# The experts' gate table moves to DRAM and is filled by indirect adding transfers

## The chip, the cores and the metric

The kernel runs on one core of one Trainium2 chip, in one launch. The metric is the device time of that core in microseconds (us). TensorE is called PE, VectorE DVE, ScalarE ACT, GpSimd POOL, and SyncE SP, as in the profile.

## The reference

Two transformer blocks, one after the other, on 256 tokens of width 2048, in float32. What matters here is the last part of the second block, `peer`: 16,384 experts, numbered by a pair of keys (128 x 128), of which each token takes 16 for each of 8 heads.

```
q  = x @ wq                                  # 8 heads x 256
s1, s2 = q[..., :128] @ keys1.T, q[..., 128:] @ keys2.T
v1, i1 = top_k(s1, 16);  v2, i2 = top_k(s2, 16)
top_s, pos = top_k(v1[:, None] + v2[None, :], 16)      # 16 of 256 candidates
expert = (i1 * 128 + i2)[pos]
gate   = softmax(top_s)
z      = x . u[expert]                       # 128 picks for each token
out    = sum over picks of gelu(z) * gate * v[expert]
```

Both kernels compute it densely. They work out z for all 16,384 experts as a matrix product (`u`), take gelu, multiply by a gate table G of [16,384 experts x 256 tokens] that is zero except at the picked places (an expert picked by two heads of one token has the sum of both gates), and multiply by all of `v`.

## The kernel before

**Stream.** All large weights come as one stream of 902 units of [128 x 1024] floats, 512 KB each. Two units are a pair. SP loads unit n into one of four slots (`raw`) as soon as the low part of unit n-4 is made (L601). ACT rounds the unit to fp32r (`w_hi`, `split_hi`, L474), DVE makes the rest (`w_lo`, `split_lo`, L483), and PE multiplies with both. ACT may write slot s only when PE has done unit n-4. The order of work is written out by hand on each engine; the helper `ahead` splits the pair that comes two after the one that PE is at.

**The u part.** Experts come in NB = 128 blocks of 128. For one block PE takes a pair: for each of the two units, 8 products of 512 columns with `w_hi` (L532) and 8 of 256 with `w_lo` (L539) (`halves_out`). ACT copies the low half of the bank (`low_half`, L545), DVE adds the other half (`add_halves`, L550), ACT takes gelu. Block pairs of PE must wait for the sum of the block two before (`wait_summed`), since two banks take turns.

**Where the blocks are made.** `wqu`: the queries of a head and two blocks of u, 8 times; POOL adds the halves (`add_copied`). `u_decode`: 16 blocks, while DVE turns the top-16 lists into experts and gates, unit by unit between its splits (`more`); at its end the gates, the first and the second index stand in `PICK`. `u_gates`: 64 blocks, while the gate table is made. `u_late`: 32 blocks. `v`: 128 pairs, 24 products of 512 columns each (`expert`, L2571 to L2573). In `v`, ACT and DVE split the next block of gated activations into `expert_hi_t` and `expert_lo_t`, and DVE makes `w_lo`.

**The gate table.** G takes all of the large buffer `big` (128 KB of each partition), as [second index x first index x token]. PE turns `PICK` (6 transposes, L2530) so that the 128 picks of a token lie on partitions. For each token POOL makes a one-hot matrix of the second index (L678), DVE a one-hot matrix of the first index times the high and the low part of the gate (L2005), and PE multiplies them (L2540, [128 x 128] by 256 columns). ACT copies the low half into G (L1145) and DVE adds the high half (L1999). Four tokens go with each of the 64 pairs of `u_gates`, between the products with `w_hi` and with `w_lo` of the second unit:

```
for s in range(4):
    pe.matmul(GATE_BANKS[n][s // 2][...], hot[:, s, :], weighted[:, s, :, :]..., start=True, stop=True)
```

**The activations.** Since G fills `big`, gelu of the first 96 blocks is stored in DRAM (`z_kept`, by ACT's queue) and read back (L1163, L1195) into two buffers `GB` in `u_late` and in the first half of `v`, where DVE multiplies it into G (L2037, L2063). The last 32 blocks are multiplied at once (L2034).

Of the kernel before, what the change touches and what calls it, by code (L numbers as in the profile page):

```python
# [28 lines left out]
F32 = mybir.dt.float32  # L29
# [6 lines left out]
P = 128  # L36
S = 256
# [28 lines left out]
SLOT_N = PH * PK  # L66

# [3 lines left out]
         ("wqu", 4 * PH), ("u_decode", 2 * PH), ("u_gates", S // 4), ("u_late", NB // 4), ("v", NB)]  # L71
EARLY = 3 * NB // 4
LATE = NB - EARLY
# [11 lines left out]
for _name, _count in [("conv", 4 * CONV_J), ("rnn", 2 * KT), ("heads", 2 * H2), ("u_decode", 2 * PH), ("u_gates", S // 4),  # L85
                      ("u_late", LATE)]:
    HALVED[_name] = _n
    _n += _count
# [5 lines left out]
for _name, _count in [("ident", P), ("iota", P), ("band", TT * 2 * P), ("causal", TT * S), ("cos", TT * HALF),  # L94
                      ("sin", TT * HALF)]:
    CONST[_name] = (_n, _n + _count)
    _n += _count
# [37 lines left out]
def build(nc, stream, x, p_t, rows, consts, params, rg_w, ukv, keys_t, out):  # L135
    ctx = ExitStack()
    with ctx:
# [24 lines left out]
        with nc.sbuf_tensor("expert_act", [P, 2, 2, S], F32R) as expert_act:  # L162
            pass
        weighted = sb("weighted", [P, 4, 2, P], F32R)
        with nc.sbuf_tensor("below_hot", [P, CONST["causal"][0]], F32), \
                nc.sbuf_tensor("hot", [P, 4, P], F32R) as hot:
            pass
# [4 lines left out]
        slot_t = sb("slot_t", [P, 3, S])  # L172
# [3 lines left out]
        z_kept = nc.dram_tensor("z_kept", (EARLY, P, S), F32, kind="Internal").ap()  # L176
# [91 lines left out]
        PICK = at(16896, 3 * SLOT_N * TT).rearrange("p (a h t k) -> p a h t k", a=3, h=PH, t=TT)  # L268
        PICKT = at(17664, 3 * SLOT_N * TT).rearrange("p (a t h k) -> p a t h k", a=3, h=PH, t=TT)
# [4 lines left out]
        G = big[:, :].rearrange("p (b t) -> p b t", b=NB)  # L274

        first_index = slot_t[:, 0, :]
        second_index = par[:, 0:S]
        gate_hi = slot_t[:, 1, :]
        gate_lo = slot_t[:, 2, :]
        GATE_BANKS = [[banks[0], banks[1]], [banks[4], banks[5]]]  # L280
        GZ = c("band").rearrange("p (s n) -> p s n", s=2)
        GB = c("causal").rearrange("p (s n) -> p s n", s=2)

# [28 lines left out]
        idx8 = stat[:, 8:16]  # L312
# [120 lines left out]
        picks_ready = sem("picks_ready")  # L433
        picks_turned = sem("picks_turned")
        slots_kept = sem("slots_kept")
        hot_turn = sem("hot_turn")
        hot1 = sem("hot1")
        hot2 = sem("hot2")
        hot_used = [sem(f"hot_used{n}") for n in range(4)]
        gate_low = sem("gate_low")  # L440
        gate_kept = [sem(f"gate_kept{n}") for n in range(2)]
        gelu_ready = [sem(f"gelu_ready{n}") for n in range(2)]
        z_saved = [sem(f"z_saved{n}") for n in range(2)]
        z_back = [sem(f"z_back{n}") for n in range(2)]
        early_ready = [sem(f"early_ready{n}") for n in range(2)]
# [77 lines left out]
        def halves_out(pe, pair, odd, bank, units=(0, 1), between=None, paced=None):  # L523

            for u in units:
# [8 lines left out]
                if u and between:  # L534
                    between()
# [20 lines left out]
        def tokens_out(pe, part, i, per, k0, outs, fills, acts=None, units=range(8)):  # L556

            high, low = acts or (act_hi, act_lo)
            for uu in units:
# [5 lines left out]
                for kk in range(2):  # L565
# [13 lines left out]
        primed = [y_made, z_saved, early_ready, scored, rg_done, logits_made, hot2, hot_used, conv_b_used,  # L579
                  conv_h_used, conv_gate_used, qi_scored, rel_used, xc_ready, th_used, gr_used, head_mixed, ps_made,  # L580
                  ps_used, act_ready, qkvg_taken_s, qkvg_taken_v, probs_kept, mix_used, added, gated, rel_ready,
                  rg_exp, k_kept, v_kept, p_exp, ga_tanh, p_kept, ps_kept, gate_kept, gelu_ready]
# [42 lines left out]
        def _(pool):  # L625
# [6 lines left out]
            pool.sem_inc(pool_summed, 4)  # L632

            with pool.Fori(0, TT) as t:
                with pool.Fori(0, KVH) as g:
# [5 lines left out]
                                     .rearrange("p o n -> p (o n)")).then_inc(staged, 1)  # L641

# [20 lines left out]
            with pool.Fori(0, PH) as h:  # L663
# [3 lines left out]
                for n in range(2):  # L667
                    add_copied(Z_HALVES[:, n, 0:S], Z_HALVES[:, n, :], h * 4 + (2 + n))
            pool.wait_ge(slots_kept, 3)
# [19 lines left out]
        def _(act):  # L689
# [369 lines left out]
            def save_early(b2, n, block):  # L1059

                act.wait_ge(z_saved[n], b2 * 16 + 1)
                act.wait_ge(pool_summed, block + 5)
                act.activation(GZ[:, n, :], Z_HALVES[:, n, 0:S], ACT.Gelu).then_inc(gelu_ready[n], 1)
                act.wait_ge(gelu_ready[n], b2 + 2)
                act.dma_start(z_kept[bass.ds(b2 * 2 + n, 1), :, :].rearrange("o p n -> (o p) n"), GZ[:, n, :])\
                   .then_inc(z_saved[n], 16)
# [1654 lines left out]
```

## Time and profile before

| | |
|---|---|
| median of 3 runs | 2732.92 us (2732.72 to 2734.38) |
| span of the profiled execution, first to last instruction | 2730.6 us |
| PE busy | 2707.6 us (99%) |
| DVE busy | 1890.1 us (69%) |
| ACT busy | 1391.3 us (51%) |
| POOL busy | 358.1 us (13%) |
| DMA | 522.17 MB, mean 191 GB/s |

The profiled execution's own time outside the profiler is not listed; its span stands 2.3 us below the median of the runs, which also takes in what lies before the first and after the last instruction. Busy time of an engine is the union of its instructions. Matmuls overlap, so the time of one (0.39 us for 512 columns) is longer than the step from one to the next (0.23 us).

### The profile page before, as it was taken

The numbers are of one execution on the slowest core, as the hardware profiler recorded it, in microseconds if no ns is written. First come the engines' busy times: TensorE is split into PE (matmuls) and PEld (weight loads), VectorE is DVE, ScalarE is ACT, GpSimd is POOL, SyncE is SP. The second block draws the span as 40 slices with busy tenths as digits, with TensorE's granted clock in tenths as the row PEclk, the third lists the DMA queues.
The fourth block names the chain that finished last, engine by engine and source line by source line (L and its number), as shares of the span: only waits on it lengthen the run. The fifth ranks groups of instructions, "written<-read, shape, count | busy, mean of one in ns | idle before, by whom it ended". The sixth has DMA issues, their size and how long they took to land.

```text
span 2730.6 us, 48285 instructions
## 1 busy us (share of the span) xinstructions
PE 2707.6 (99%) x14430; PEld 2332.0 (85%) x14430; DVE 1890.1 (69%) x3047; ACT 1391.3 (51%) x2118; POOL 358.1 (13%) x422
## 2 busy tenths in 40 slices
PE   8999999999999999999999999999999999999998
PEld 7888888898888888888888888888888888888887
DVE  6666665668986666479997888886665555555555
ACT  6455445556665444465455555554544444444444
POOL 0000000000001111011104666660000000000000
PEclk9999999999999999999999999999999999999999
DMA  6544455454554444555565555556666666655564
GB/s 256 192 155 160 148 196 184 176 215 162 172 176 159 155 159 140 200 193 195 196 199 202 197 190 197 194 196 206 211 215 217 218 213 218 212 194 192 194 239 156
DMA packets 162487, 522.17 MB, mean 191 GB/s; under 512 B 18048, under 2 KB 42880, under 8 KB 161408
## 3 DMA queue, kind: packets, MB, share of 16 engines
q1 hardware_dynamic: 131472, 478.35, 51.0%
q10 hardware_dynamic: 30960, 43.14, 4.5%
q8 instruction: 29, 0.48, 0.1%
q14 instruction: 26, 0.21, 0.0%
HBM read 504.63 MB, written 16.78 MB: 191 GB/s over the span
## 4 chain that ended last, share of the span: by engine, by line
PE 94%; DVE 3%; ACT 1%; issue 1%; DMA 0%; SPq 0%; ACTq 0%; DVEq 0%
PE bank L532 31%; PE bank L539 16%; PE bank L2571 8%; PE bank L2573 8%; PE bank L2572 8%; PE bank L572 4%; PE bank L574 4%; PE bank L573 4%; PE bank L2540 1%; PE bank L2373 1%; PE bank L2368 1%; DVE w_lo L483 1%; PE bank L506 1%; PE bank L507 1%; PE bank L508 1%
## 5 line engine op out<-in xcount | busy, mean ns | idle before, releaser
L483 DVE TENSOR_TENSOR w_lo<-raw,w_hi 128x1024 fp32r<-128x1024 f32 x902 | 1095.0, 1224 | 694.7 <-ACT w_hi L474 683.4
L474 ACT ACTIVATE w_hi<-raw 128x1024 fp32r<-128x1024 f32 x902 | 952.1, 1060 | 943.1 <-PE bank L539 359.8
L532 PE MATMUL bank<-act,w_hi 128*128 128x512 f32 x3840 | 975.8, 396 | 2.3 <-DVE big L1420 1.1
L532 PEld LDWEIGHTS bank<-act,w_hi 128*128 128x128 f32 x3840 | 692.6, 189 | 133.7 <-issue 7.2
L539 PEld LDWEIGHTS bank<-act,w_lo 128*128 128x128 f32 x3840 | 520.0, 191 | 33.1
L539 PE MATMUL bank<-act,w_lo 128*128 128x256 f32 x3840 | 535.8, 282 | 0.0
L2571 PE MATMUL bank<-w_hi,expert_act 128*128 128x512 f32 x1008 | 392.6, 389 | 0.1
L2573 PE MATMUL bank<-w_hi,expert_act 128*128 128x512 f32 x1008 | 392.5, 389 | 0.0
L2572 PE MATMUL bank<-w_lo,expert_act 128*128 128x512 f32 x1008 | 392.4, 389 | 0.0
L678 POOL TENSOR_SCALAR hot<-cst,stat 128x128 fp32r<-128x128 f32 x256 | 255.1, 1011 | 129.1 <-PE bank L2540 128.7
L2571 PEld LDWEIGHTS bank<-w_hi,expert_act 128*128 128x128 f32 x1008 | 189.3, 188 | 39.5 <-DVE cst L550 0.5
L2573 PEld LDWEIGHTS bank<-w_hi,expert_act 128*128 128x128 f32 x1008 | 189.3, 188 | 39.2
L2572 PEld LDWEIGHTS bank<-w_lo,expert_act 128*128 128x128 f32 x1008 | 189.3, 188 | 39.1
L572 PE MATMUL bank<-w_hi,act 128*128 128x512 f32 x320 | 126.0, 394 | 1.5 <-DVE w_lo L483 0.8
L574 PE MATMUL bank<-w_hi,act 128*128 128x512 f32 x320 | 124.8, 390 | 0.0
L573 PE MATMUL bank<-w_lo,act 128*128 128x512 f32 x320 | 124.6, 389 | 0.0
L684 POOL TENSOR_TENSOR big<-big 128x1024 f32<-128x1024 f32 x2 | 5.8, 2878 | 874.9 <-DVE big L2078 874.9
L2005 DVE SCALAR_TENSOR_TENSOR weighted<-cst,slot_t 128x256 fp32r<-128x256 f32 x256 | 116.0, 511 | 0.0
L646 POOL TENSOR_TENSOR big<-big 128x256 f32<-128x256 f32 x16 | 11.1, 696 | 485.0 <-DVE big L550 485.0
L572 PEld LDWEIGHTS bank<-w_hi,act 128*128 128x128 f32 x320 | 60.1, 188 | 15.7 <-DVE w_lo L483 1.3
L574 PEld LDWEIGHTS bank<-w_hi,act 128*128 128x128 f32 x320 | 60.1, 188 | 12.6
L573 PEld LDWEIGHTS bank<-w_lo,act 128*128 128x128 f32 x320 | 60.1, 188 | 12.1
(332 smaller groups left out, 2518.1 us busy)
## 6 DMA issues: line engine op xcount, KB each, us to landing
raw<-in_stream SPq DMA_DIRECT2D x902, 512.0 KB, 3.7
z_kept<-cst ACTq DMA_DIRECT2D x96, 128.0 KB, 2.1
cst<-z_kept ACTq DMA_DIRECT2D x96, 128.0 KB, 4.0
big<-in_ukv ACTq DMA_DIRECT2D x16, 512.0 KB, 4.6
big<-in_rows ACTq DMA_DIRECT2D x3, 1024.0 KB, 5.5
big<-in_x SPq DMA_DIRECT2D x2, 1024.0 KB, 9.7
big<-in_rg_w ACTq DMA_DIRECT2D x1, 2048.0 KB, 11.2
x_kept<-big ACTq DMA_DIRECT2D x1, 2048.0 KB, 8.3
```

The lines of the kernel that those rows point to most:

```text
L474: act.activation(w_hi[:, s, :], raw[:, s, :], ACT.Copy).then_inc(hi_ready, 1)
L483: dve.tensor_tensor(w_lo[:, s, :], raw[:, s, :], w_hi[:, s, :].bitcast(F32), ALU.subtract).then_inc(lo_ready, 1)
L532: pe.matmul(bank[:, :], w_hi[:, s, kk * P:(kk + 1) * P], act2[:, k, :, :].rearrange("p a n -> p (a n)"), start=(k == 0), stop=False)
L539: mm = pe.matmul(bank[:, 0:S], w_lo[:, s, kk * P:(kk + 1) * P], act_hi[:, k, :], start=False, stop=(k == KT - 1))
L572: pe.matmul(outs[t], a_hi, hi, start=(k == 0), stop=False)
L573: pe.matmul(outs[t], a_hi, lo, start=False, stop=False)
L574: mm = pe.matmul(outs[t], a_lo, hi, start=False, stop=(k == KT - 1))
L678: pool.tensor_scalar(hot[:, s % 4, :], iota, idx8[:, s:s + 1], None, ALU.is_equal)\
L2005: dve.scalar_tensor_tensor(out=weighted[:, s, :, :], in0=iota.unsqueeze(1).broadcast_to([P, 2, P]), scalar=first_index[:, bass.ds(tok, 1)] ...
L2571: pe.matmul(o, a_hi, hi, start=first, stop=False, skip_group_check=True)
L2572: pe.matmul(o, a_hi, lo, start=False, stop=False, skip_group_check=True)
L2573: mm = pe.matmul(o, a_lo, hi, start=False, stop=False, skip_group_check=True)
```

## The change

The table of gates is a DRAM tensor `g_kept` of 128 x 128 x 256 floats (16.8 MB), one float for each expert and token.

* **Zeroing.** POOL clears a tile of [128 x 1024] once. In the attention of the first block, in each of the 8 turns of POOL's loop, it issues 4 stores of 512 KB of that tile, 32 in all, into `g_kept`.
* **Index and gate.** DVE works out `SLOT_INDEX` = (first index * 128 + second index) * 256 + token and `SLOT_GATE`. PE's transposes, DVE's three copies to `PICKT` and ACT's four copies are gone.
* **Filling.** POOL issues 256 indirect transfers, one for each head, half of the tokens and place in the top 16. Each takes one gate from each of the 128 partitions and adds it to the float of `g_kept` at that partition's index. All 32 transfers of a head must have landed before the next head's first.
* **Activations.** gelu(z) of every block stays in `big` (`z_block`); `z_kept` is gone, with its 96 stores and 96 loads on ACT's queue.
* **Gating.** POOL loads the gate block (128 KB) of each of the 128 blocks into one of two buffers `GB`. DVE multiplies it in (`gate_block`) two blocks at a time: the first two ahead of its turn 46 of the 48 of `u_rest`, the next two in that turn, and all others in `v`.
* **Stages.** `u_gates` (64 pairs) and `u_late` (32) become `u_rest` (96 pairs), without the one-hot products. The order of the blocks changes so that blocks 16 to 31 are made beside the queries and 0 to 15 in `u_decode`.

The diff, cut to its core:

```
-         ("wqu", 4 * PH), ("u_decode", 2 * PH), ("u_gates", S // 4), ("u_late", NB // 4), ("v", NB)]
+         ("wqu", 4 * PH), ("u_decode", 2 * PH), ("u_rest", NB - 4 * PH), ("v", NB)]
...
+        SLOT_INDEX = slot_t[:, 0, :].bitcast(U32)
+        SLOT_GATE = slot_t[:, 1, :]
+        g_zero = g_kept.rearrange("(p c n) o -> c p (n o)", p=P, n=ZERO_W)
+        g_block = g_kept.rearrange("(b p n) o -> b p (n o)", b=NB, p=P)
...
 # POOL
+            pool.memset(zeros[:, :], 0.0).then_inc(zero_made, 1)
+            pool.wait_ge(zero_made, 1)
             with pool.Fori(0, TT) as t:
                 with pool.Fori(0, KVH) as g:
...
+                    for q in range(ZERO_DMAS // (TT * KVH)):
+                        pool.dma_start(g_zero[bass.ds(u * (ZERO_DMAS // (TT * KVH)) + q, 1), :, :]
+                                       .rearrange("o p n -> (o p) n"), zeros[:, :]).then_inc(zeroed, 16)
...
-            with pool.Fori(0, S // 8) as i:
-                pool.wait_ge(hot2, i * 8 + 1)
-                pool.tensor_copy(idx8, second_index[:, bass.ds(i * 8, 8)]).then_inc(g_step, 1)
-                pool.wait_ge(g_step, i + 1)
-                for s in range(8):
-                    pool.wait_ge(hot_used[s % 4], i * 2 + s // 4 + 1)
-                    pool.sem_inc(hot_turn, 1)
-                    pool.tensor_scalar(hot[:, s % 4, :], iota, idx8[:, s:s + 1], None, ALU.is_equal)\
-                        .then_inc(hot2, 1)
+            pool.wait_ge(zeroed, 16 * ZERO_DMAS)
+            pool.wait_ge(slots_ready, TT)
+            for h in range(PH):
+                if h:
+                    pool.wait_ge(scattered, 16 * TT * PK * h)
+                for i in range(h * TT * PK, (h + 1) * TT * PK):
+                    pool.indirect_dma_start(g_kept, bass.IndirectOffsetOnAxis(ap=SLOT_INDEX[:, i:i + 1], axis=0),
+                                            SLOT_GATE[:, i:i + 1], None, compute_op=ALU.add).then_inc(scattered, 16)
+            pool.wait_ge(scattered, 16 * TT * PK * PH)
+            for n in range(2):
+                pool.dma_start(GB[:, n, :], g_block[n, :, :]).then_inc(g_back[n], 16)
+            with pool.Fori(1, NB // 2) as i:
+                for n in range(2):
+                    pool.wait_ge(act_ready[n], i)
+                    pool.dma_start(GB[:, n, :], g_block[bass.ds(i * 2 + n, 1), :, :].rearrange("o p n -> (o p) n"))\
+                        .then_inc(g_back[n], 16)
...
 # ACT
+            def rest_turn(i, first=False):
                 for n in range(2):
+                    ahead(split_hi, act, "u_rest", i, 2, n)
+                    wait_summed(act, block_of("u_rest", i, 2, n - 1))
+                    act.wait_ge(unit_done, 2 * pair_of("u_rest", i, 2, n) + 2)
+                    low_half(act, z_block(i * 2 + (4 * PH + n)), banks[2 + n])
+                    gelu(2 * PH - 1 if first and not n else i * 2 + (4 * PH + n - 1))
+            def expert_hi(b, n, i, done):
+                act.wait_ge(unit_done, done)
+                act.wait_ge(act_ready[n], i + 1)
+                act.activation(expert_hi_t[:, n, :], z_block(b), ACT.Copy).then_inc(eh_ready, 1)
...
 # DVE
-            step(dve.tensor_tensor(PICK[:, 2, :, :, :].rearrange("p h t k -> p (h t) k"), cv,
+            step(dve.tensor_tensor(SLOT_GATE.rearrange("p (n k) -> p n k", k=PK), cv,
                                    crec.unsqueeze(2).broadcast_to([P, PH * TT, PK]), ALU.mult))
+            step(dve.scalar_tensor_tensor(out=picked[1], in0=picked[0], scalar=float(KEYS), in1=picked[1],
+                                          op0=ALU.mult, op1=ALU.add))
             step.wait()
-            for a in range(3):
-                ins = dve.tensor_copy(PICKT[:, a, :, :, :].rearrange("p t h k -> p h t k"), PICK[:, a, :, :, :])
+            for t in range(TT):
+                dve.tensor_scalar(SLOT_INDEX.rearrange("p (h t k) -> p h t k", h=PH, t=TT)[:, :, t, :],
+                                  PICK[:, 1, :, t, :], float(S), c("token")[:, t:t + 1], ALU.mult, ALU.add)\
+                   .then_inc(slots_ready, 1)
...
+            def gate_block(b, n, i):
+                dve.wait_ge(gelu_ready, b + 1)
+                dve.wait_ge(g_back[n], i * 16 + 16)
+                z = z_block(b)
+                dve.tensor_tensor(z, z, GB[:, n, :], ALU.mult).then_inc(act_ready[n], 1)
...
+            with dve.Fori(0, REST // 2 - 2) as i:
+                rest_turn(i)
+            dve.wait_ge(gelu_ready, 4 * PH)
+            for n in range(2):
+                gate_block(n, n, 0)
+            rest_turn(REST // 2 - 2)
+            for n in range(2):
+                expert_lo(n, n, n + 1)
+                gate_block(2 + n, n, 1)
+            rest_turn(REST // 2 - 1)
...
+            with dve.Fori(0, NB // 2 - 2) as i:
                 for n in range(2):
                     next_expert(i, n)
+                    gate_block(i * 2 + (4 + n), n, i + 2)
...
 # PE
-            for a in range(3):
-                pe.wait_ge(picks_ready, a + 1)
-                for t in range(TT):
-                    pe.transpose(banks[4 + a][:, t * P:(t + 1) * P],
-                                 PICKT[:, a, t, :, :].rearrange("p h k -> p (h k)"),
-                                 ident).then_inc(picks_turned, 1)
...
-            with pe.Fori(0, S // 8) as i:
-                for n in range(2):
-                    pe.wait_ge(gelu_ready[n], i + (2 * PH + 1))
-                    halves_out(pe, pair_of("u_gates", i, 2, n), odd_of("u_gates", n), banks[2 + n], between=lambda: four_tokens(i, n))
-            with pe.Fori(0, LATE // 2) as i:
+            with pe.Fori(0, REST // 2) as i:
                 for n in range(2):
-                    wait_summed(pe, block_of("u_late", i, 2, n - 2))
-                    halves_out(pe, pair_of("u_late", i, 2, n), odd_of("u_late", n), banks[2 + n])
+                    wait_summed(pe, block_of("u_rest", i, 2, n - 2))
+                    halves_out(pe, pair_of("u_rest", i, 2, n), odd_of("u_rest", n), banks[2 + n])
```

## Rows read from the trace of the kernel before

**Rows 1.** The page: span, busy time of PE, and the chain that ended last.

```profile
span 2730.6 us, 48285 instructions
...
PE 2707.6 (99%) x14430; PEld 2332.0 (85%) x14430; DVE 1890.1 (69%) x3047; ACT 1391.3 (51%) x2118; POOL 358.1 (13%) x422
...
PE 94%; DVE 3%; ACT 1%; issue 1%; DMA 0%; SPq 0%; ACTq 0%; DVEq 0%
```

**Rows 2.** Busy time by stretch: attention; u_gates; u_late; halves of v.

```profile
core 0: us, PE busy (x) PEld busy (x) DVE busy (x) ACT busy (x) POOL busy (x), PEclk, DMA share, GB/s
...
141.00:332.00 191.00, 191.00 (x1163) 167.22 (x1162) 128.72 (x200) 94.70 (x173) 11.92 (x16) 1.00 0.45 157
...
1463.00:1851.00 388.00, 387.96 (x2303) 345.33 (x2304) 332.44 (x572) 215.75 (x383) 257.73 (x283) 1.00 0.55 194
1851.00:2026.00 175.00, 174.84 (x1004) 153.88 (x1003) 111.38 (x158) 88.38 (x127) 0.00 (x0) 1.00 0.62 212
2026.00:2376.00 350.00, 349.95 (x1545) 289.68 (x1544) 200.29 (x259) 157.02 (x195) 0.00 (x0) 1.00 0.64 216
```

**Rows 3.** PE in order of time, one pair of u_gates apart: start, duration.

```profile
1602.67 0.64 PE L2540 MATMUL bank<-weighted,hot 128*128 128x256 f32 x4
...
1608.73 0.64 PE L2540 MATMUL bank<-weighted,hot 128*128 128x256 f32 x4
```

**Rows 4.** PE in order of time, one pair of u_late apart.

```profile
1903.05 2.00 PE L532 MATMUL bank<-act,w_hi 128*128 128x512 f32 x8
...
1908.64 2.00 PE L532 MATMUL bank<-act,w_hi 128*128 128x512 f32 x8
```

**Rows 5.** PE in order of time: transposes, start of u_gates, start of v.

```profile
1443.11 2.00 PE L532 MATMUL bank<-act,w_hi 128*128 128x512 f32 x8
1444.95 1.11 PE L539 MATMUL bank<-act,w_lo 128*128 128x256 f32 x8
1445.91 0.82 PE L2530 MATMUL bank<-cst,big 128*128 128x128 f32 x6
1446.48 2.10 PE L532 MATMUL bank<-act,w_hi 128*128 128x512 f32 x8
...
1457.75 2.00 PE L532 MATMUL bank<-act,w_hi 128*128 128x512 f32 x8
...
2025.96 0.40 PE L2571 MATMUL bank<-w_hi,expert_act 128*128 128x512 f32 x1
```

**Rows 6.** DVE in order of time: the last steps of the decoding.

```profile
1433.31 0.42 DVE L1981 TENSOR_TENSOR big<-big,stat 128x256 f32<-128x256 f32 x1
...
1433.77 0.70 DVE L1985 COPY big<-big 128x256 f32<-128x256 f32 x3
```

**Rows 7.** One line each: one-hot on POOL, and POOL's smallest copy.

```profile
L678 POOL TENSOR_SCALAR hot<-cst,stat x256: 601/843/1647, 1449.1 to 1842.1; 128x128 fp32r<-128x128 f32 x128
...
L673 POOL COPY stat<-par x32: 189/190/192, 1448.6 to 1831.8; 128x8 f32 x32
```

**Rows 8.** One line each: DMA issues of ACT's queue, store and load.

```profile
L1135 ACTq DMA_DIRECT2D z_kept<-cst x64: 339/343/356, 1469.0 to 1850.1; - x64
...
DMA to landing us min/median/max: 1.8/2.0/3.2
...
DMA to landing us min/median/max: 2.0/4.2/5.0
```

**Rows 9.** The page: DMA queues: packets, MB, share of 16 engines.

```profile
q1 hardware_dynamic: 131472, 478.35, 51.0%
q10 hardware_dynamic: 30960, 43.14, 4.5%
```

**Rows 10.** In order of time: low part made, and the split four units on.

```profile
1898.85 1.23 DVE L483 TENSOR_TENSOR w_lo<-raw,w_hi 128x1024 fp32r<-128x1024 f32 x1 [0.59 <-ACT w_hi L474]
...
1908.84 1.06 ACT L474 ACTIVATE w_hi<-raw 128x1024 fp32r<-128x1024 f32 x1 [0.76 <-PE bank L539]
```

**Rows 11.** Stream loads, issue to landing; POOL's waits in the attention.

```profile
DMA to landing us min/median/max: 3.0/3.7/11.3
...
POOL big L639 <- PE bank L2224: 153.2, 7, 24.7
```

**Rows 12.** Groups: DVE's gate multiplication in v.

```profile
L2063 DVE TENSOR_TENSOR big<-cst,big 128x256 f32 x64 | 26.8, 418 | 0.0
```

More of the change, by code:

```diff
@@ L84 @@
 _n = 0
-for _name, _count in [("conv", 4 * CONV_J), ("rnn", 2 * KT), ("heads", 2 * H2), ("u_decode", 2 * PH), ("u_gates", S // 4),
-                      ("u_late", LATE)]:
+for _name, _count in [("conv", 4 * CONV_J), ("rnn", 2 * KT), ("heads", 2 * H2), ("u_decode", 2 * PH),
+                      ("u_rest", REST)]:
     HALVED[_name] = _n
@@ L1057, in keep_early, with early_gelu @@
                 copy_halves(Z_HALVES[:, n, :], banks[2 + n], pair, block, before)
[L1059 to L1061 removed]
+            def early_gelu(b2, n, block):
                 act.wait_ge(pool_summed, block + 5)
[L1063 to L1066, printed above, removed]
+                act.wait_ge(added[1], 9)
+                z = z_block(b2 * 2 + (2 * PH + n))
+                act.activation(z, z, ACT.Gelu).then_inc(gelu_ready, 1)
             def router_turn(h, first=False):
@@ L1115, in _ @@
-            early_turn(0, first=True)
+                    low_half(act, z_block(i * 2 + n), banks[2 + n])
+                    if not (first and not n):
+                        gelu(i * 2 + (n - 1))
+            decode_turn(0, first=True)
             with act.Fori(1, PH // 2) as i:
-                early_turn(i)
+                decode_turn(i)
             act.wait_ge(pick_diff, 1)
             act.activation(CV, CV, ACT.Exp).then_inc(pick_exp, 1)
-            with act.Fori(PH // 2, PH - 1) as i:
-                early_turn(i)
@@ L1138, in gates_turn @@
-            def gates_turn(i, first=False):
-                for n in range(2):
-                    ahead(split_hi, act, "u_gates", i, 2, n, units=(0,))
-                    if not (first and not n):
-                        save_gelu(i, n - 1)
-                    for half in range(2):
-                        act.wait_ge(hot_used[2 * half + 1], i * 2 + n + 2)
-                        act.activation(G[:, :, bass.ds(i * 8 + (4 * n + 2 * half), 2)],
-                                       GATE_BANKS[n][half].rearrange("p (t a b) -> p a b t", t=2, a=2)[:, 1, :, :],
-                                       ACT.Copy).then_inc(gate_low, 1)
-                    ahead(split_hi, act, "u_gates", i, 2, n, units=(1,))
-                    act.wait_ge(unit_done, 2 * pair_of("u_gates", i, 2, n) + 2)
-                    act.wait_ge(z_saved[n], i * 16 + (32 * PH + 1))
-                    low_half(act, GZ[:, n, :], banks[2 + n])
@@ L1173, in expert_hi @@
[L1173 to L1185 removed]
+            with act.Fori(PH // 2, PH) as i:
+                decode_turn(i)
@@ L1187, in next_experts @@
+            rest_turn(0, first=True)
+            with act.Fori(1, REST // 2 - 1) as i:
+                rest_turn(i)
+            for n in range(2):
+                expert_hi(n, n, 0, 2 * FIRST["u_rest"])
+            rest_turn(REST // 2 - 1)
+            wait_summed(act, block_of("u_rest", REST // 2 - 1, 2, 1))
+            gelu(NB - 1)
             def next_experts(i):
@@ L1926, in next_low @@
                 if u:
-                    add_halves(dve, GZ[:, pair % 2, :], banks[2 + pair % 2], block_of("u_decode", 0, 2, pair))
+                    add_halves(dve, Z[:, pair, :], banks[2 + pair % 2], block_of("u_decode", 0, 2, pair))
             def more(count=1):
@@ L2011, in gates_turn @@
-            def gates_turn(i, last=False):
-                for n in range(2):
-                    ahead(split_lo, dve, "u_gates", i, 2, n, units=(0,))
-                    if not (last and n):
-                        four_tiles(i, n + 1)
-                    ahead(split_lo, dve, "u_gates", i, 2, n, units=(1,))
-                    add_halves(dve, GZ[:, n, :], banks[2 + n], block_of("u_gates", i, 2, n))
-                    add_gates(i, n)
-            four_tiles(0, 0)
-            with dve.Fori(0, S // 8 - 1) as i:
-                gates_turn(i)
@@ L2023, in _, with rest_turn @@
[L2023 to L2037 removed]
+            def rest_turn(i):
+                for n in range(2):
+                    ahead(split_lo, dve, "u_rest", i, 2, n)
+                    add_halves(dve, z_block(i * 2 + (4 * PH + n)), banks[2 + n], block_of("u_rest", i, 2, n))
```

224 lines of the change are left out of this document (49 added, 175 removed).

## The prediction

> **What bounds the kernel now.** The page comes first: PE is busy 2707.6 of 2730.6 us and makes 94% of the chain that ended last [rows 1]. So only what leaves PE's own list, or makes PE wait, moves the time. The table by stretches says the same of the stages in question: in u_gates PE is busy 387.96 of 388 us, in u_late 174.84 of 175, in the first half of v 349.95 of 350, and the granted clock is 1.00 in all of them, the higher of the two levels (2.4 GHz) [rows 2]. DVE comes nearest, with 332 of 388 us in u_gates and 111 of 175 in u_late. POOL works 258 us in u_gates and nothing after it. The sum is made against the span of 2730.6 us; the median of the runs, 2732.92, lies 2.3 us above it, and I carry that over unchanged.
>
> **What leaves PE.** A pair of u_gates takes 1608.73 - 1602.67 = 6.06 us, a pair of u_late without one-hot products 1908.64 - 1903.05 = 5.59 [rows 3, 4]. With 64 pairs that is 64 x 0.47 = 30.1 us. The same from the ends: from the first product of u_gates to the first of v are 2025.96 - 1457.75 = 568.2 us [rows 5]; 96 pairs of 5.59 are 536.6, so 31.6 us go if all 96 run at the pace of u_late. The 1.5 us between the two are the start of u_gates, where PE waits for the first one-hot tiles, and the passage to u_late, where ACT waits for its last store; both causes are removed, and I take 31.6. The six transposes stretch one unit of 2.79 us (half a pair) from 1443.11 to 1446.48, 3.37 us, so 0.6 more goes [rows 5]. Sum: 32.2 us off PE.
>
> **What leaves the other engines.** On DVE 256 tiles and 128 additions, on ACT 128 copies, 192 DMA issues of 0.34 us [rows 8], on POOL 256 one-hots of 0.6 to 1.6 us [rows 7]. Worth nothing: PE covers them. Should PE's cover have been incomplete, u_late (same u work, DVE at 64%) shows that the lighter load keeps PE's pace.
>
> **What is added on DVE and ACT.** Three index operations of 128 to 256 elements take the place of three copies of together 0.70 us [rows 6]: nothing, and the list is ready at about 1434.8. ACT's low half now comes behind the second split in u_decode, as it does in u_late, where PE still has its 5.59. In v, DVE does one multiplication of 0.42 us for each of the 128 pairs [rows 12]; before it did one in each of the first 64 and PE did not wait there (349.95 of 350). In the second half it is new, but makes the load that of the first half: nothing. DVE also loses u_late's two multiplications a pair.
>
> **What is added on POOL and the DMA queues: gate blocks.** 128 loads of 128 KB. The same size landed in 4.2 us from ACT's queue, at most 5.0 [rows 8]. A buffer comes free at one multiplication and is needed again two pairs (about 11 us) later. Even with 3 us more for an issue from POOL, an allowance of mine, it fits. If not, DVE waits, with the next w_lo behind it, and PE behind that. Nothing is taken; a price if cover fails is 128 / 2 x 1 us for each us by which a load is over 10.
>
> **Zeroing.** 16.8 MB in 8 bursts of 2 MB between 141 and 332 us, where the DMA share is 0.45 and PE has no idle time [rows 2]. POOL waits up to 24.7 us a turn there for PE [rows 11]; behind its four issues are queued the two copies of the next turn, for which the attention scores on PE wait. Four issues at 0.34 us are 1.4 us, at 4.2 us each 17: under 24.7 both ways. The stream has slack: the low part of a unit ends at 1900.1, which releases SP's next load, and the split that needs it starts at 1908.8 [rows 10], so 8.7 us against a median landing of 3.7 [rows 11]. A burst would have to double the landing time. Bounds: 0 and, at 3 us a burst, 24 us. I take 1 us, near the lower, as 5 us of slack stand against it.
>
> **The 256 indirect adding transfers: the term that decides.** No row of this trace shows a DMA issued by POOL. First the time they have. They start at 1434.8. DVE meets the first gate block ahead of turn 46, when PE begins pair 92 of u_rest: u_rest starts at 1457.75 - 0.6 = 1457.2, so 1457.2 + 92 x 5.59 = 1971.5. Behind the waiting multiplication are queued the w_lo of pairs 94 and 95 and the sums that free PE's banks. The weights of pairs 92 and 93 are already split, so PE goes on for 11.2 us; two multiplications and a w_lo take 2.1 of these. The deadline is about 1980.5. From 545.7 us go one load of 4.2 and eight drains (one for each head) of a store's 2.0 us [rows 8], which leaves 525.5 us, or 2.05 us for each transfer. PE's gain is spent when the mean is 2.05 + 32.2 / 256 = 2.18 us.
>
> Bounds for one: below, the issue on ACT's queue, 0.34 us [rows 8] (87 us in all). Above, one at a time from issue to landing: 4.2 us (1075 us). Between ends far apart I look for the nearest work: POOL going over 128 elements, 0.84 us median and 1.65 at most [rows 7], since it must form 128 addresses. I take 1.2 us: 256 x 1.2 + 16 + 4 = 327 us, done at about 1762, some 218 us early, and DVE does not wait. The term is 0.
>
> POOL's own rows vary from 601 to 1647 ns for one and the same operation, while DVE reads two tiles beside it [rows 7]. The Trainium skill says in "SBUF — State Buffer", "Who interferes with whom", that a DVE instruction with two SBUF inputs contends with a GpSimd instruction that reads SBUF; the trace agrees in that spread. By it the reading of indices could be slowed to the upper end, 1.65 us, which is still under 2.05, and the sum stays.
> The page "DMA: Bandwidth & Descriptors", "Anatomy of one DMA — SWDGE (gpsimd) path", of the Trainium skill puts about 2.0 us on a DMA as fixed cost; no run here shows it yet. If none overlapped, the estimate is 512 us, just inside the window.
>
> **Total.** 2732.9 - 32.2 + 1 = 2701.7, rounded 2702 us.
>
> **Rivals.**
> *A transfer costs too much* (slower; decides from 2.05 us, a net loss from 2.18). Place: DVE's wait ahead of turn 46; PE stands from about 1982. Each 0.1 us is 25.6 us. At 2.5 us it gives 2702 + 0.45 x 256 = 2817, at 4.2 us 2702 + 550 = 3252. For it: nothing in the trace shows such a transfer cheaper, they add (read and write back in DRAM), and each names 128 separate floats. Against: more than 200 us of margin at the value taken, and within a head no transfer waits for the one before. Chance 0.22.
> *One read for each index.* If POOL fetches the 128 indices one by one, each at its smallest copy's 0.19 us [rows 7], a transfer takes 24 us, and the time is 2702 + 256 x 24.3 - 525 = about 8400 us. Against it: POOL's operations over 128 partitions take all partitions at once. Chance 0.03.
> The Trainium skill warns of this in "GPSIMD Engine Reference", "Performance pitfalls for Q7 kernels": about 102 cycles for each small read command, such as one for each gather index, without overlap; no run here shows it.
> *The DMA engines fill up.* ACT's queue paid 0.045 x 16 x 2730.6 / 30960 = 64 ns of an engine for a packet [rows 9]. 256 x (128 + 16) packets at that price are 146 us of each engine. The stream and z_kept had 0.55 to 0.62 of the engines [rows 2], about 0.57 x 537 = 306 us over u_rest. 452 of 537 us fits; with two packets for each float (read, then write) it is 598, and u_rest is stretched by 61 us: 2763. Signs would be PE waiting for ACT, and ACT for `raw`. Chance 0.12, spread over 2702 to 2763: 0.07 faster, 0.01 the same, 0.04 slower.
> *The zeroing bursts delay the stream or the copies of the attention.* 2708 to 2726. Chance 0.02.
>
> **How the numbers follow.** The forecast, all hidden, has 0.61, with a range of its own of 2696 to 2708 (the 1.5 us of passages and the 1 us of zeroing each way, and some us of new small waits). A measurement of this kernel can tell about 0.2%, 5.5 us, from no change. Faster: 0.61 + 0.07 + 0.02 = 0.70. Slower: 0.22 less 0.02 that falls within or below the bound, plus 0.03 and 0.04, 0.27. The same: 0.03. For 8 in 10 I take 2696 to 2800: nearly all of the forecast (0.59), the full DMA engines (0.12), the bursts (0.02), and of the costly transfers the part up to (2800 - 2702) / 256 + 2.05 = 2.43 us each (0.08).
>
> **What the changed profile would show.** Right: u_rest in 537 us, 5.59 for each pair, no L2540; POOL's last indirect transfer well before 1970; DVE without a wait for a DMA ahead of the first gate block; v at its old pace. Wrong: PE idle in one piece of tens of us at the end of u_rest, with DVE's multiplication waiting for the load of `GB` from `g_kept` (transfers too slow); many small waits of ACT for `raw` in u_rest (full DMA engines); pairs of v longer than before (gate loads late). The steps I am least sure of are the 1.2 us and the packets of one float.

## The result and the profile after

The changed kernel takes 2929.91 us (2927.37 to 2931.53, 4 runs) beside 2732.82 (2732.18 to 2734.38, 4 runs) for the one before: a ratio of 1.072, 95% interval 1.0705 to 1.0735. The forecast of 2702 us and its range are missed. The answer to [rows 1] and [rows 9] on the page of the kernel after:

```profile
span 2930.0 us, 46164 instructions
...
PE 2677.3 (91%) x14168; PEld 2301.0 (79%) x14168; DVE 1734.9 (59%) x2662; ACT 1343.6 (46%) x1988; POOL 632.2 (22%) x551
...
PE   8999999999999999999999999990008999999998
...
q1 hardware_dynamic: 131472, 478.35, 50.5%
q0 software_dynamic: 47616, 33.71, 7.1%
...
PE 69%; POOL 15%; issue 11%; DVE 3%; DMA 1%; ACT 1%; DVEq 0%; SPq 0%; ACTq 0%; POOLq 0%
...
L669 POOL DMA_INDIRECT g_kept<-slot_t x256 | 448.2, 1751 | 387.5 <-issue 305.1
...
g_kept<-zeros POOLq DMA_DIRECT2D x32, 512.0 KB, 5.7
cst<-g_kept POOLq DMA_DIRECT2D x128, 128.0 KB, 3.4
```

PE has 30.3 us less work than before, so the gain is there. But three of the forty slices are empty on PE, one hole in one place, and POOL with "issue" makes 26% of the chain that ended last. The windows of u_rest, of the middle of the hole, and of two stretches of v, with the attention ahead of them, answer to [rows 2]:

```profile
core 0: us, PE busy (x) PEld busy (x) DVE busy (x) ACT busy (x) POOL busy (x), PEclk, DMA share, GB/s
141.00:332.00 191.00, 191.00 (x1162) 167.17 (x1161) 129.24 (x201) 94.10 (x173) 28.92 (x48) 1.00 0.70 246
1457.00:1971.00 514.00, 514.00 (x2946) 452.39 (x2945) 256.18 (x276) 248.17 (x368) 292.49 (x158) 1.00 0.70 188
1985.00:2200.00 215.00, 0.00 (x0) 0.00 (x0) 0.00 (x0) 0.00 (x0) 130.99 (x85) 0.50 0.17 0
2240.00:2376.00 136.00, 136.00 (x602) 112.65 (x601) 78.04 (x100) 60.74 (x76) 13.44 (x25) 1.00 0.70 217
2376.00:2710.00 334.00, 334.00 (x1475) 276.69 (x1474) 191.65 (x245) 148.74 (x184) 33.36 (x62) 1.00 0.70 217
```

In each of these windows but the hole's PE has no idle time. In the hole only POOL works: it is still issuing transfers. The waits say who hangs on whom (engine, line, releaser: total, times, longest):

```profile
DVE big L1951 <- DMA cst<-g_kept: 234.2, 1, 234.2
PE bank L522 <- DVE big L538: 230.7, 4, 229.5
...
POOL big L629 <- PE bank L2134: 118.9, 7, 22.6
...
POOL g_kept L669 <- issue: 305.1, 248, 3.2
```

DVE stands once, for the load of the first gate block; PE stands for the sum that is queued on DVE behind it. On DVE in order of time:

```profile
1973.56 0.41 DVE L538 TENSOR_TENSOR big<-big,bank 128x256 f32 x1
...
2208.14 0.98 DVE L1951 TENSOR_TENSOR big<-big,cst 128x256 f32<-128x256 f32 x2 [234.17 <-DMA cst<-g_kept]
```

And on PE, two rows one pair of u_rest apart (5.59 us, as in [rows 4]), then the hole:

```profile
1903.97 2.00 PE L522 MATMUL bank<-act,w_hi 128*128 128x512 f32 x8
...
1909.56 2.00 PE L522 MATMUL bank<-act,w_hi 128*128 128x512 f32 x8
...
1981.23 1.11 PE L527 MATMUL bank<-act,w_lo 128*128 128x256 f32 x8
2211.86 3.78 PE L522 MATMUL bank<-act,w_hi 128*128 128x512 f32 x8 [229.51 <-DVE big L538]
```

What fills POOL's time is seen in its own order of time, from the first transfer on:

```profile
1434.14 1.81 POOL L669 DMA_INDIRECT g_kept<-slot_t  x1 [66.00 <-DVE slot_t L1934]
1436.26 2.41 POOL L669 DMA_INDIRECT g_kept<-slot_t  x1 [0.30 <-issue]
1438.98 1.58 POOL L669 DMA_INDIRECT g_kept<-slot_t  x1 [0.30 <-issue]
1443.70 1.56 POOL L669 DMA_INDIRECT g_kept<-slot_t  x1 [3.15 <-issue]
1445.57 1.61 POOL L669 DMA_INDIRECT g_kept<-slot_t  x1 [0.31 <-issue]
1447.48 2.35 POOL L669 DMA_INDIRECT g_kept<-slot_t  x1 [0.30 <-issue]
1452.59 1.57 POOL L669 DMA_INDIRECT g_kept<-slot_t  x1 [2.76 <-issue]
```

Three issues, then a stand: idle time of about 2.5 us that the profile puts down to no wait ("issue"). Numbered from 0, POOL stands ahead of transfers 3, 6, 7, 9, 12, 14, 15, 18, 21, and so on: every multiple of 3 or of 7, save where a drain (the wait for all transfers of a head) falls on it. That makes 106 stands of 2.47 us in the mean (1.81 to 3.21), about as long as one of the seven drains (16.4 / 7 = 2.3). The last transfer starts at 2202.29. From first start to last end are 769.7 us: 448.2 of work (256 x 1.751), 16.4 in the drains, and 305.1 of "issue". Of the last, 248 gaps of 0.30 make 74, and 231 is what the stands add. Per transfer: 1.75 + 0.29 + 0.90, and 0.06 of drains, together 3.01 us. The forecast had 1.2.

### The profile page after: what moved, and what is told of

Its sections match the earlier page's. It is cut to its first block, busy times and chain, and to the rows that moved or that the text cites. A ratio compares the mean times of both kernels' runs of the same rounds, so it can differ in the third digit from the quotient of the medians.

```text
span 2930.0 us, 46164 instructions
## 1 busy us (share of the span) xinstructions
PE 2677.3 (91%) x14168; PEld 2301.0 (79%) x14168; DVE 1734.9 (59%) x2662; ACT 1343.6 (46%) x1988; POOL 632.2 (22%) x551
## 4 chain that ended last, share of the span: by engine, by line
PE 69%; POOL 15%; issue 11%; DVE 3%; DMA 1%; ACT 1%; DVEq 0%; SPq 0%; ACTq 0%; POOLq 0%
PE bank L522 17%; POOL g_kept L669 15%; PE bank L527 8%; PE bank L2457 8%; PE bank L2458 8%; PE bank L2459 8%; PE bank L560 4%; PE bank L562 4%; PE bank L561 4%; DMA g_kept<-slot_t 1%; PE bank L2283 1%; PE bank L2278 1%; DVE w_lo L473 1%; PE bank L496 1%; PE bank L497 1%
## 5 line engine op out<-in xcount | busy, mean ns | idle before, releaser
L669 POOL DMA_INDIRECT g_kept<-slot_t x256 | 448.2, 1751 | 387.5 <-issue 305.1
L677 POOL DMA_DIRECT2D cst<-g_kept x126 | 67.8, 538 | 619.5 <-DVE big L1951 619.2
L533 ACT ACTIVATE big<-bank 128x256 f32<-128x256 f32 (+1 forms) x208 | 76.0, 365 | 254.3 <-DVE big L538 228.5
L1951 DVE TENSOR_TENSOR big<-big,cst 128x256 f32 (+1 forms) x128 | 53.6, 419 | 234.3 <-DMA cst<-g_kept 234.2
L654 POOL TENSOR_TENSOR big<-big 128x256 f32<-128x256 f32 (+1 forms) x32 | 33.0, 1032 | 247.8 <-ACT big L1052 247.8
L538 DVE TENSOR_TENSOR big<-big,bank 128x256 f32<-128x256 f32 (+1 forms) x208 | 85.4, 414 | 0.0
```

What stands on the lines that cost most here:

```text
L538: dve.tensor_tensor(dest, dest, bank[:, 0:S], ALU.add).then_inc(summed, 1)
L669: pool.indirect_dma_start(g_kept, bass.IndirectOffsetOnAxis(ap=SLOT_INDEX[:, i:i + 1], axis=0), SLOT_GATE[:, i:i + 1], None, compute_op=AL ...
```

## The experiments

All times are medians, ratios are to the kernel before on the same chip.

**1. Half of the transfers** (`half_transfers`). Leaves out every second transfer, so half of the gates are missing from the table; the counts of the waits are halved with it, and all else is as in the kernel after.

```
-                for i in range(h * TT * PK, (h + 1) * TT * PK):
+                for i in range(h * TT * PK, (h + 1) * TT * PK, 2):
...
-            pool.wait_ge(scattered, 16 * TT * PK * PH)
+            pool.wait_ge(scattered, 8 * TT * PK * PH)
```

> Leaves out every second of the 256 adding transfers (so half of the gates are missing); everything else is the changed kernel. Theory A (only the transfers' term was mis-sized, the rest of the sum holds): 128 transfers at the 3.0 us of the changed kernel's trace take 390 us, are hidden, and the time is 2702 us (2698 to 2708). Theory B (the change also loads u_rest or v in another way): more than 2710 us.

Measured: 2700.38 us, ratio 0.9883 (0.9868 to 0.9897); span 2699.1. With the transfers done by 1838 (128 of them, last issue at 1835.6), nothing is left of the hole. So every other part of the change together gives -31.9 us (2732.28 for the kernel before on the same chip), and the whole loss of the kernel after is its hole: 2700.4 + 229.5 = 2929.9.

**2. More room for descriptors** (`room_1088`, `room_2048`, `room_4096`). One number at the launch, the size that is set aside for the descriptors of POOL's transfers. In the last, index and gate lie in a tile of the constants that is free by then, to make room in SBUF.

```
-    nc = bacc.Bacc("TRN2", ..., dynamic_dma_scratch_size=1024)
+    nc = bacc.Bacc("TRN2", ..., dynamic_dma_scratch_size=2048)   # 1088, 4096
```

> The changed kernel with 1088 instead of 1024 bytes of a partition for the descriptors of POOL's transfers. In the trace of the changed kernel POOL issues in groups of at most three with 0.3 us between, then stands 2 to 3 us. Theory A (the room for descriptors holds three adding transfers, and POOL waits for room): the groups grow to four, the mean step falls from 3.2 to about 2.8 us while DVE works, and the time falls by some 60 to 100 us to 2830 to 2870. Theory B (the DMA engines need about 3 us for an adding transfer, whatever the room): the mean step stays, 2930 us.

> The changed kernel with 2048 bytes for the descriptors. Theory A (room): groups of about seven, the step falls to 2.15 us (issue 1.85 with DVE at work, 0.30 between) plus a seventh of one stand, 2.15 to 2.5 us; the last lands 25 to 110 us behind the deadline of 1980, time 2727 to 2811 us. Theory B (the DMA engines set the pace): 2930 us.

> The changed kernel with 4096 bytes for the descriptors; the index and gate tile lies in the constants' band tile, unused by then, to make the space. Theory A (room): 2.15 to 2.32 us a transfer, time 2720 to 2765 us. Theory B (the DMA engines set the pace): 2930 us.

Measured: 1088: two runs, 2913.33 and 3012.33; too far apart for a verdict. The expected groups of four did not come: the 106 stands lie ahead of the same transfers as at 1024, to the last one. 2048: 2839.65, ratio 1.0393 (1.0378 to 1.0408). 4096: three runs at 2824.67 to 2825.26 and three at 2866.91 to 2868.94, for which I have no cause; the median, 2846.09, lies between the two, and the ratio is 1.039 (1.0335 to 1.0445). The trace is of a run of 2825.23. POOL in order of time in `room_2048`, a group of seven between two stands, two of it left out:

```profile
1710.92 2.43 POOL L669 DMA_INDIRECT g_kept<-slot_t  x1 [2.88 <-issue]
1713.66 2.48 POOL L669 DMA_INDIRECT g_kept<-slot_t  x1 [0.30 <-issue]
1716.44 2.49 POOL L669 DMA_INDIRECT g_kept<-slot_t  x1 [0.30 <-issue]
1719.24 2.49 POOL L669 DMA_INDIRECT g_kept<-slot_t  x1 [0.30 <-issue]
...
1727.64 2.48 POOL L669 DMA_INDIRECT g_kept<-slot_t  x1 [0.31 <-issue]
1732.87 1.55 POOL L669 DMA_INDIRECT g_kept<-slot_t  x1 [2.75 <-issue]
```

Now the stands lie ahead of the multiples of 7, 35 of them, and at 4096 ahead of those of 15 and of 28, 25 of them. So their number goes by the room. What they add falls from 231 to 80 us and to 55 (issue 154.4 and 128.9, less 74). Their length stays (2.56 and 2.44 us in the mean): the one ahead of 1732.87 takes 2.75 us, though the first transfer of its group was issued 20 us earlier. It is as if POOL waited each time for all that it had issued, not for the oldest. But the issue itself grows from 1.75 to 1.99 and 2.02 us, and takes back 60 to 70 us. So both times missed theory A, which had at most 2811 us for `room_2048` and 2765 for `room_4096`. The row to look at is the 2.48: its step, 2.79 us, is one unit of PE, half a pair. In `room_4096`, DVE and POOL in order of time show what it keeps step with:

```profile
1855.47 1.23 DVE L473 TENSOR_TENSOR w_lo<-raw,w_hi 128x1024 fp32r<-128x1024 f32 x1 [1.57 <-ACT w_hi L464]
...
1855.63 2.49 POOL L669 DMA_INDIRECT g_kept<-cst  x1 [0.30 <-issue]
...
1858.26 1.23 DVE L473 TENSOR_TENSOR w_lo<-raw,w_hi 128x1024 fp32r<-128x1024 f32 x1 [1.24 <-ACT w_hi L464]
1858.43 2.48 POOL L669 DMA_INDIRECT g_kept<-cst  x1 [0.30 <-issue]
```

Each issue begins 0.16 us into DVE's subtraction, which reads `raw` and `w_hi`, both in SBUF, and ends 0.14 us before the next subtraction. So the theory became: the issue itself is slowed beside that subtraction.

**3. Plain writes** (`plain_writes`). Leaves out the adding: where two heads pick the same expert for a token, the later gate stays alone. Size 1024 as in the kernel after.

```
-    SLOT_GATE[:, i:i + 1], None, compute_op=ALU.add).then_inc(scattered, 16)
+    SLOT_GATE[:, i:i + 1], None).then_inc(scattered, 16)
```

> The changed kernel (1024 bytes for the descriptors) with plain writes in place of adding transfers; left out is the sum where two heads of a token pick one expert. Theory A (an adding transfer takes about twice the room of a plain one, since it reads its target too): groups of seven in place of three, and about 2.4 to 2.6 us a transfer while DVE works, 2820 to 2850 us. Theory B (the room is counted in transfers, or an add costs nothing more): groups of three, 2930 us.

Measured: 2700.38 us (2 runs), ratio 0.9882 (0.9864 to 0.99), where both theories had 2820 us or more. At 1024 bytes the stands lie ahead of the multiples of 7 alone, 35 of them, as in `room_2048`; those of 3 are gone. This was expected; they are longer, 3.14 us in the mean. That the issue falls too was not expected, and it is what makes the time. The transfers' line, the kernel after first and `plain_writes` second (duration ns min/median/max, first and last start):

```profile
L669 POOL DMA_INDIRECT g_kept<-slot_t x256: 1554/1570/2607, 1434.1 to 2202.3; - x128
```

```profile
L669 POOL DMA_INDIRECT g_kept<-slot_t x256: 964/978/2018, 1435.0 to 1914.2; - x128
```

An adding transfer costs 1.55 us of POOL at least, a plain one 0.96. My 1.2 us from [rows 7] would have been near the mean issue of a plain one (1.12), but not near its mean step (1.88).

**4. The subtraction without its pair of SBUF inputs** (`lo_without_sbuf_pair`). `room_4096`, but in turns 0 to 45 of u_rest DVE's subtraction reads its second input from a PSUM bank, so these low parts hold something else; its length stays (1.22 us).

```
-    dve.tensor_tensor(w_lo[:, s, :], raw[:, s, :], w_hi[:, s, :], ALU.subtract)
+    dve.tensor_tensor(w_lo..., raw..., banks[6]..., ALU.subtract)
```

> 4096 bytes for the descriptors, and in turns 0 to 45 of u_rest DVE's subtraction that makes w_lo takes its second input from a PSUM bank instead of w_hi; so the low parts are not those of the weights there. Number and length of DVE's instructions stay. Theory A (POOL's issue is held up by DVE instructions with two inputs in SBUF): the issue falls from 2.17 us to 1.56 us at all times, a transfer takes 2.04 us, the last lands at about 1975, and the time is 2700 to 2712 us. Theory B (any work of DVE, or the DMA load, holds it up): the issue stays 2.17 us and the time 2825 to 2846 us.

Measured: 2726.3 us (seven runs at 2719.59 to 2726.56, three at 2746.89 to 2749.9), ratio 0.9998 (0.9973 to 1.0023). The time missed both theories. The issue did what theory A said, but stands (61 us) and drains (19 us) are left, 0.31 us for each transfer. The mean step is 2.18 us instead of 2.04, and DVE still waits 21.4 us for the first gate blocks. In order of time:

```profile
1807.36 1.56 POOL L669 DMA_INDIRECT g_kept<-cst  x1 [0.30 <-issue]
1808.47 1.22 DVE L1946 TENSOR_TENSOR w_lo<-raw,bank 128x1024 fp32r<-128x1024 f32 x1 [1.24 <-ACT w_hi L464]
...
1809.22 1.56 POOL L669 DMA_INDIRECT g_kept<-cst  x1 [0.30 <-issue]
```

The issue at 1809.22 begins while DVE subtracts, and still takes 1.56 us; the median of all 256 went from 1.99 to 1.56, and none of the 106 that begin inside such a subtraction takes more than 1.58. Except for that input, program, operation and length on DVE are those of `room_4096`: the slowing is the pair of SBUF inputs. The Trainium skill says in "SBUF — State Buffer", "Who interferes with whom", that a DVE instruction with two SBUF inputs contends with a GpSimd instruction that reads SBUF. The trace agrees, 1.56 against 2.48 us. The same section infers that `tensor_tensor` leaves descriptor generation alone. The traces do not speak against that, for they show which part of the issue is held up: its start. Two pairs of rows of the kernel after:

```profile
1550.60 1.23 DVE L473 TENSOR_TENSOR w_lo<-raw,w_hi 128x1024 fp32r<-128x1024 f32 x1 [1.24 <-ACT w_hi L464]
1550.78 2.48 POOL L669 DMA_INDIRECT g_kept<-slot_t  x1 [0.30 <-issue]
...
1558.85 1.57 POOL L669 DMA_INDIRECT g_kept<-slot_t  x1 [2.80 <-issue]
1558.98 1.23 DVE L473 TENSOR_TENSOR w_lo<-raw,w_hi 128x1024 fp32r<-128x1024 f32 x1 [1.57 <-ACT w_hi L464]
```

The first issue begins inside a running subtraction and takes 2.48 us; the second begins 0.13 us before one, runs beside nearly all of it, and takes 1.57. Over the whole trace, 78 of the 256 issues begin at least 0.05 us inside a subtraction with more than 0.12 us of it to go. Each takes, to within 0.1 us, 1.56 us plus what is left of that subtraction, less 0.12. None of the other 178 takes more than 1.58.

In `room_2048` and `room_4096` 133 and 137 issues begin so, and this is the growth of 60 to 70 us. It also explains the step: an issue that begins 0.17 us into a subtraction takes 1.56 + 1.06 - 0.12 = 2.50 us, and with the gap of 0.30 the next one begins at the same place of the next subtraction. What the issue reads at its start was not tested, but direct transfers, which have no indices, are spared. Of the 160 direct issues of POOL in the kernel after, 28 begin so, and take 0.53 to 0.55 us, as nearly all others do. The line of most of them:

```profile
L677 POOL DMA_DIRECT2D cst<-g_kept x126: 536/536/552, 2209.3 to 2893.6; - x126
```

**5. The same with nothing left out** (`hi_copy_in_psum`, `hi_copy_gates_later`). ACT writes w_hi a second time into PSUM that is free in u_rest, DVE subtracts that copy. The second kernel also makes the first two gate multiplications one turn later.

```
+    act.wait_ge(lo_ready, 2 * pair + u - 1)
+    act.activation(hi_in_psum(u).bitcast(F32R), raw[:, s, :], ACT.Copy).then_inc(hp_ready, 1)
...
-    dve.tensor_tensor(w_lo[:, s, :], raw[:, s, :], w_hi[:, s, :], ALU.subtract)
+    dve.tensor_tensor(w_lo[:, s, :], raw[:, s, :], hi_in_psum(u), ALU.subtract)
```

> As a full version: 4096 bytes for the descriptors; in turns 0 to 45 of u_rest ACT writes the rounded weights a second time, into PSUM banks that are free there, and DVE subtracts that copy. ACT then works about 5.0 of 5.59 us for each pair. Theory A (DVE's second SBUF input): 2700 to 2712 us, faster than both kernels. Theory A but ACT too full: PE waits for w_hi in u_rest, pairs of more than 5.59 us, up to 2730 us. Theory B: 2825 us or more.

> The same with DVE's first gate multiplications two pairs (11.2 us) later, ahead of turn 47. Theory A: the wait that may be left at the deadline, 0 to 10 us, goes, and 2700 to 2703 us are left; against that, a late first block of experts may cost 1 to 2 us at the start of v. Theory B: 11 us below the run without the shift, 2814 us or more.

Measured: 2723.62 us, ratio 0.9965 (0.9953 to 0.9977), and 2715.16, ratio 0.9937 (0.9924 to 0.9951). Both lie above what theory A gave (2700 to 2712 and 2700 to 2703), for the reason of 4: stands and drains are left. The issue is 1.56 us again; ACT pays 1.01 us for each of 184 copies and PE's pairs stay at 5.59. The later gates shorten DVE's wait from 26.8 to 17.1 us: the deadline moves with the turn.

**6. Order of the transfers** (`copy_and_order`, `copy_order_gates_later`, `order_only`). Head 0 writes plainly, since the table holds zeros and no expert comes twice in a head. Each half of the tokens has its own semaphore, so a head waits only for the same half of the head before, which has had half a head's time to land. With the copy of 5, with copy and later gates, and without the copy. The two parts of this edit were not measured apart.

```
+    for t in range(TT):
+        if h:
+            pool.wait_ge(scattered[t], 16 * PK * h)
+        ...
+            add = dict(compute_op=ALU.add) if h else {}
```

> A full version from what the runs showed: 4096 bytes for the descriptors, the rounded weights a second time in PSUM, the first head with plain writes (its table is all zero then), and one semaphore for each half of the tokens, so that a head waits only for the same half of the head before, which was issued 16 transfers earlier. Gates at their old place. Theory A (the size of the transfers' term decides everything): against the copy in PSUM alone, 32 x 0.58 = 19 us and seven drains of about 2 us go, the last transfer starts at about 1963, in front of the deadline of 1980, and the time is 2700 to 2704 us, 1.1% faster than the kernel before. Theory B (some other loss is in those versions, such as ACT's load or the contents of v): 2710 us or more.

> The same with the first gate multiplications two pairs later. Theory A: nothing is left to wait for, so it is the same as without the shift, 2700 to 2704 us, or 1 to 2 us slower by a late start of v. Theory B: 2710 us or more.

> 4096 bytes for the descriptors, first head with plain writes and one semaphore for each half of the tokens, but without the copy in PSUM, so that DVE's subtraction has both inputs in SBUF. Theory A: the issue is 2.17 us again for adding ones, and the 2846 us of 4096 bytes alone fall by 19 + 15 to about 2790 to 2812 us, still slower than the kernel before. Theory B (the stands between heads were what cost): under 2733 us.

Measured: 2700.67 us, ratio 0.9881 (0.9865 to 0.9898); 2701.09, ratio 0.9882 (0.9866 to 0.9899); without the copy 2795.15, ratio 1.0247 (1.0212 to 1.0283). The groups of POOL's transfers (busy, mean ns, idle before), with the copy and without it:

```profile
L693 POOL DMA_INDIRECT g_kept<-cst x256 | 382.9, 1496 | 179.2 <-issue 113.2
```

```profile
L671 POOL DMA_INDIRECT g_kept<-cst x256 | 521.5, 2037 | 175.9 <-issue 109.9
```

The idle time is the same: in both the drains are gone and 14 stands are left of 25, ahead of the transfers 47, 63, 79 and so on, the last of each half head from the third on. Only the issue differs, by 0.54 us. The copy alone is worth 94 us here. All three times lie in the ranges of theory A. `copy_and_order` leaves nothing out and is 1.2% faster than the kernel before, 7.8% faster than the one after.

**All kernels by one sum.** In the kernel after, PE's last product ahead of the hole ends at 1982.3 and its next starts 9.6 us after the last transfer's start (2202.3 to 2211.9). So a last start up to 1972.7 is hidden, and beyond that the span is 2699.1 + (last start - 1972.7). A step is (last start - first start) / 255.

| kernel | bytes | issue, median us | step, us | last start | sum | span |
|---|---|---|---|---|---|---|
| after | 1024 | 1.57 | 3.01 | 2202.3 | 2928.7 | 2930.0 |
| `room_2048` | 2048 | 1.80 | 2.66 | 2112.6 | 2839.0 | 2840.1 |
| `room_4096` | 4096 | 1.99 | 2.59 | 2095.2 | 2821.6 | 2823.6 |
| `order_only` | 4096 | 2.48 | 2.47 | 2065.0 | 2791.4 | 2793.5 |
| `hi_copy_in_psum` | 4096 | 1.56 | 2.20 | 1996.5 | 2722.9 | 2724.6 |
| `lo_without_sbuf_pair` | 4096 | 1.56 | 2.18 | 1990.2 | 2716.6 | 2718.0 |
| `copy_and_order` | 4096 | 1.56 | 1.94 | 1929.1 | 2699.1 | 2699.0 |
| `plain_writes` | 1024 | 0.98 | 1.88 | 1914.2 | 2699.1 | 2699.0 |

(In `order_only` a median above the mean step comes from the 32 plain writes and the issues that do not begin inside a subtraction.) One number, the time at which POOL starts its last transfer, gives all eight spans to 2.1 us.

## Why the prediction was wrong

The step that failed is the sentence "I take 1.2 us" for one indirect adding transfer, under "The 256 indirect adding transfers". It measured 3.01 us from start to start, 2.94 without the drains. The mechanism, the place, the deadline and the threshold were those of the rival *A transfer costs too much*: by its own rule 2702 + (2.94 - 2.05) x 256 = 2930 us, and 2929.91 came. It had 0.22, and the range ended at 2.43 us a transfer.

What was wrong in that choice is of two kinds.
- The value came from an operation that only resembles the work: POOL going over 128 elements [rows 7]. Its median of 0.84 us lies near the 0.96 of a plain issue. The 1.2 us taken lie below the 1.56 that an adding one takes undisturbed.
- The sum knew two ways to pay, all overlapped or none. The real one lies between: three issued one after the other, then a full stop. No term stood for that, and the stands were 0.90 of the 3.01 us. The slowing beside DVE was named, with 1.65 us as its end; it reached 2.6 us, though in the mean it was only 0.19 (1.75 less 1.56).

That end was a misreading of [rows 7], which do not show what DVE does beside POOL. In order of time the trace of the kernel before does:

```profile
1641.89 1.23 DVE L483 TENSOR_TENSOR w_lo<-raw,w_hi 128x1024 fp32r<-128x1024 f32 x1 [0.32 <-ACT w_hi L474]
1641.94 1.65 POOL L678 TENSOR_SCALAR hot<-cst,stat 128x128 fp32r<-128x128 f32 x1
```

POOL's one-hot takes 0.60 us undisturbed, and here 0.60 plus the 1.18 left of the subtraction, less 0.12, or 1.66 against 1.65 measured. So the 1.65 is no ceiling for any operation: the slowing adds up to 1.05 us to what the operation takes. On the 1.2 us taken it would have given 2.25 at the worst, beyond the 2.05 that the prediction allowed.

The other steps, one by one:
- **PE -32.2 us.** `half_transfers` gives -31.9 together with the zeroing, for which 1 us was added: -31.2 in the forecast. Pairs take 5.59 us, v starts 31.5 us earlier there (1994.47 against 2025.96).
- **DVE and ACT at nothing, low half behind the second split.** PE is busy 514.00 of 514 us of u_rest.
- **Gate blocks at nothing.** The median landing is 3.4 us (I had 4.2, at most 5.0, and an allowance of 3), and in v PE is busy 136.00 of 136 and 334.00 of 334.
- **Zeroing 1 us.** It cost nothing that shows: an issue takes 0.53 us and a 512 KB store 5.7 us to land; PE is busy 191.00 of 191 in the attention, and POOL's longest wait for PE there is 22.6 us for 24.7 before [rows 11]. The burst rival is out.
- **Deadline 1980.5.** PE ended at 1982.3, with DVE in turn 46, in front of the first gate block.
- **Drains 8 x 2.0 us.** 16.4 us in seven, and 1.8 for the last.
- **One read for each index (24 us each)** is out: the whole undisturbed issue is 1.56 us.
- **The DMA engines fill up** is out. In the hole 85 transfers alone give a DMA share of 0.17, so one takes 0.17 x 215 / 85 = 0.43 us of each engine, 110 us for all (my price gave 146), and in u_rest the share is 0.70.

Left open: why 1088 bytes act as 1024, what POOL waits for in a stand, why the stands of `order_only` and `copy_and_order` lie where they do, and why `room_4096` has two times, 2825 and 2868 us.

## What to carry to other kernels

When work moves to a queue that no row of the trace has used, its term needs three parts: the issue, how many may be issued between two stops, and what the issue shares with its neighbours. Each must be bounded alone, and the upper end must combine them. A slowing that is the rest of another engine's instruction is added to the time of the work, so its end is not the longest row seen. Work out the last start that is still hidden (here 2.11 us a transfer) before believing in a margin, and when the price is unknown within a factor of two of it, put the weight on both sides. If such a hole shows, look first at the rhythm of the issues: here stands ahead of every n-th meant room, a step equal to another engine's meant contention, and each had an edit of a few lines that tests it.

## What was not expected of the hardware

- Transfers of 128 single floats issued by POOL: 1.56 us of POOL each when they add in DRAM, 0.96 when they write, and 0.30 between two.
- An indirect issue that begins inside a DVE subtraction with two SBUF inputs waits for its end, up to 1.05 us more; one that begins 0.13 us before it takes 1.57 us. Direct issues of POOL stay at 0.53 to 0.55 us there.
- POOL comes to a full stop of about 2.5 us ahead of every multiple of 3 and of 7 adding transfers at 1024 bytes, of 7 at 2048, of 15 and of 28 at 4096, and of about 3.1 us ahead of every 7 plain ones at 1024. The Trainium skill gives in "DMA: Bandwidth & Descriptors", "The descriptor swizzle", 9 read and 9 write descriptors for each engine for a transfer of 1 MiB to 128 partitions, and in "Terms" 16 bytes for one. As an estimate from that page, if a transfer of 128 floats names as many, 1024 bytes are 64 places and hold seven plain transfers (63), 4096 bytes hold 28 (252). The 7 and 28 agree. The 3, 7 and 15 would be 17 places a transfer, as if an adding one named its 8 targets twice on one side; the runs do not show that, and 68 places at 1088 bytes should then hold four. Nor is it a rule for all orders: in `order_only` and `copy_and_order`, at 4096 bytes, 32 plain transfers go without a stop where 28 should fill the room. Their stops fit 28 and 15 only if the count begins again at each half head, where the semaphore changes, and no run tests that.
- After 229.5 us without work the granted clock was 0.50 (the lower level, 1.2 GHz), and PE's first eight products of 512 columns took 3.78 us, the next eight of them 1.99.
